# A prompt-and-sample decoder step: input rows and first norm in another order, the samples' depthwise convolution as 32x32 matmuls

## What is computed

```python
mods = (silu(c) @ w_ada + b_ada).reshape(B, N_MOD, D_MODEL)
...
h = modulate(x, norm_g[l, 0], m[:, 0], m[:, 1])
...
def conv_module(h, prev, w_pw1, b_pw1, w_dw, b_dw, ln_g, ln_b, w_pw2):
    a = h @ w_pw1 + b_pw1
    u = a[..., :D_MODEL] * jax.nn.sigmoid(a[..., D_MODEL:])
    up = jnp.concatenate([prev.astype(u.dtype), u], axis=1)
    y = lax.conv_general_dilated(up, w_dw[:, None, :].astype(up.dtype), (1,), 'VALID',
                                 dimension_numbers=('NWC', 'WIO', 'NWC'),
                                 feature_group_count=D_MODEL) + b_dw
    y = jax.nn.silu(layernorm(y, ln_g, ln_b))
    return y @ w_pw2, up[:, -(CONV_W - 1):]
```

## Time and profile before

| | us |
|---|---|
| median of 3 runs | 1905.48 (1901.27 to 1909.15) |
| the profiled execution | 1907.56 |
| its span, first to last instruction | 1905.9 |
| PE busy | 1679.4 |
| DVE busy | 914.8 |
| ACT busy | 561.5 |
| POOL busy | 270.9 |
| SP's DMA queue | 172.54 MB |

### The profile page before, as it was taken

The page is one execution under the profiler, slowest core; times in us unless marked ns, Lnnn a source line. Parts: engine busy times, 40 slices in busy tenths (PEclk is TensorE's granted clock), DMA queues, the critical chain, the costliest instruction groups (busy, mean ns, idle before and its releaser), DMA issues.

```text
span 1905.9 us, 30256 instructions
## 1 busy us (share of the span) xinstructions
PE 1679.4 (88%) x12409; PEld 1488.9 (78%) x12409; DVE 914.8 (48%) x1618; ACT 561.5 (29%) x1058; POOL 270.9 (14%) x384
## 2 busy tenths in 40 slices
PE   5788874497999999997988989988897999999995
PEld 2666653397999999997887965454497999999994
DVE  1479999755323232335224246756645323223333
ACT  2332221333222122222221355544423222122222
POOL 1002939120000000000210034432300000000000
PEclk8899987698999999998899999978998999999997
DMA  9399983051233222321322240020221233222311
GB/s 311 157 348 341 307 278 102 0 137 56 78 97 92 66 79 85 107 64 34 100 73 56 77 121 23 1 68 23 67 68 55 78 95 94 63 82 82 110 32 50
DMA packets 236591, 198.10 MB, mean 104 GB/s; under 512 B 6999, under 2 KB 196127, under 8 KB 236253
## 3 DMA queue, kind: packets, MB, share of 16 engines
q1 hardware_dynamic: 230448, 172.54, 29.4%
q0 software_dynamic: 5840, 23.30, 3.9%
q10 hardware_dynamic: 173, 0.39, 0.1%
HBM read 188.88 MB, written 11.20 MB: 105 GB/s over the span
## 4 chain that ended last, share of the span: by engine, by line
PE 71%; DVE 11%; issue 8%; ACT 4%; DMA 3%; DVEq 1%; POOL 1%; SPq 1%; ACTq 0%; POOLq 0%
PE ps L1444 58%; PE ps L1426 4%; PE ps L1752 2%; PE ps L1705 2%; DMA ada<-in_w_ada_dram 2%; DVE y L1117 2%; DVE wl L971 1%; PE ps L1631 1%; DVE r L1117 1%; PE ps L1472 1%; DVE r L995 1%; PE ps L1822 1%; DVE y L1122 1%; PE ps L1607 1%; DVE t L1005 1%
## 5 line engine op out<-in xcount | busy, mean ns | idle before, releaser
L1444 PE MATMUL ps<-Hh,wh 128*128 128x288 f32 x2128 | 470.8, 304 | 67.9 <-DVE Hl L1010 40.8
L1444 PE MATMUL ps<-Hl,wh 128*128 128x288 f32 x2128 | 465.4, 301 | 0.0
L1444 PE MATMUL ps<-Hh,wl 128*128 128x288 f32 x2128 | 464.2, 300 | 0.0
L646 ACT ACTIVATE wh<-raw 128x1024 fp32r<-128x1024 f32 (+1 forms) x173 | 192.9, 1116 | 828.2 <-PE ps L1444 805.8
L1444 PEld LDWEIGHTS ps<-Hh,wh 128*128 128x128 f32 x2128 | 351.5, 194 | 71.9 <-issue 70.5
L1444 PEld LDWEIGHTS ps<-Hl,wh 128*128 128x128 f32 x2128 | 351.9, 193 | 0.2
L1444 PEld LDWEIGHTS ps<-Hh,wl 128*128 128x128 f32 x2128 | 351.5, 193 | 0.2
L971 DVE TENSOR_TENSOR wl<-raw,wh 128x1024 fp32r<-128x1024 f32 (+1 forms) x173 | 225.1, 1301 | 255.5 <-ACT wh L646 255.0
L1444 PE MATMUL ps<-ah,wl 128*128 128x288 f32 x704 | 150.8, 296 | 0.0
L1444 PE MATMUL ps<-ah,wh 128*128 128x288 f32 x704 | 150.8, 296 | 0.0
L1444 PE MATMUL ps<-al,wh 128*128 128x288 f32 x704 | 150.7, 296 | 0.0
(11 more groups left out here) (273 smaller groups left out, 1958.5 us busy)
## 6 DMA issues: line engine op xcount, KB each, us to landing
ada<-in_w_ada_dram SPq DMA_DIRECT2D x64, 1024.0 KB, 7.6
raw<-in_ffn_w_up_dram SPq DMA_DIRECT2D x88, 512.0 KB, 3.8
raw<-in_ffn_w_down_dram SPq DMA_DIRECT2D x32, 704.0 KB, 4.6
raw<-in_conv_w_pw_dram SPq DMA_DIRECT2D x24, 512.0 KB, 8.5
raw<-in_w_kv_dram SPq DMA_DIRECT2D x12, 512.0 KB, 3.7
C<-in_cache_kv_dram POOLq DMA_DIRECT2D x32, 128.0 KB, 4.1
raw<-in_nsa_w_in_dram SPq DMA_DIRECT2D x8, 512.0 KB, 3.8
Cs<-in_cache_kv_dram SPq DMA_DIRECT2D x16, 256.0 KB, 3.9
```

The costliest lines, as they stand in the source:

```text
L646: A(wh[:, u % RING, 0:K, 0:w], raw[:, u % RING, 0:K, 0:w], ACT.Copy).then_inc(hi_ready, 1)
L1444: last = M(ps[0:w, 2 * s + h, 0:HT], wt[:, s, k, 0:w], rt[:, k, h * HT:(h + 1) * HT], start=(k == 0 and i == 0), stop=(k == K - 1 and i == 2))
```

## The change

**First stage.** Five row buffers in place of two (`ROW_BUF`, the new `xrows`), so that POOL issues all five blocks of x at once. The blocks of `state_conv` follow. PE turns all five blocks ahead of strip 0, and sums the squares between strip 0 and strip 1, into banks 4 and 5 (`stats0`) in place of 6 and 7. ACT's and DVE's first splits of weights move behind the blocks of x. `norm(0)` takes the reciprocal ahead of its wait for `mods`. The two copies from HBM to HBM (`conv_sample`, `win_sample`) move on POOL's queue behind the first unit of the second projection.

**Convolution.** `sel32` holds 1 where the partition is the column plus a multiple of 32. POOL builds, for each chunk, a tensor `taps_t[cc]` of 32 slots by 32 columns: slot k is `sel32` times tap k, so that each group of 32 partitions holds a 32x32 diagonal; slot 31 holds the bias and meets a row of ones. Chunks 0 and 1 are built early, into `stage`; 2 to 7, into the room of `Hh` and `Hl`, once PE has done the 16 units. PE then runs 32 x 32 x 64 matmuls, 4 partition groups x 4 column groups x 8 rounds for each chunk, 1024 in all; the four column groups take four taps at a time, the partition groups go to banks 0 to 3. ACT copies the four banks to `parts` (128x2048), four matmuls with `sel32` add the four column groups, and ACT puts the sum into y. PE's channel sums and DVE's subtraction wait for that (`cs_ev`).

Core of the diff:

```diff
-SMP_CONV = [(0, 4), (4, 7)]
+TAPS = CW + 1
+TAPS_EARLY = 2
...
-STRIP_BLOCKS = [1, 2, 3, 4]
+
+
+ROW_BUF = [0, 1, 2, 3, 4, 0, 1]
...
+        xrows = at("xrows", [P, 3, D], rH + DC * T * 4)
...
+        taps_t = [at(f"taps{cc}", [P, TAPS, 32], off_) for cc, off_ in enumerate(
+            [rG + 4096 * cc for cc in range(TAPS_EARLY)] + [rH + 4096 * cc for cc in range(DC - TAPS_EARLY)])]
+        parts = at("parts", [P, 4, 512], rH + 4096 * (DC - TAPS_EARLY))
+        assert 4096 * (DC - TAPS_EARLY) + 8192 <= 2 * DC * T * 4
...
             def load_rows(bk):
-                n = xi_rows[bk]
-                if bk >= 2:
-
-                    pool.wait_ge(S("xi_pe"), bk - 1)
+                if bk >= 5:
+                    pool.wait_ge(S("xi_pe"), bk - 4)
                 if bk < 4:
                     src = a["x_prompt"][0, bk * P:(bk + 1) * P, :]
                 elif bk == 4:
                     src = a["x_sample"].rearrange("b t d -> (b t) d")
                 else:
                     src = a["state_conv"].rearrange("l b t d -> (l b t) d")[120 * (bk - 5):120 * (bk - 4), :]
-                pool.dma_start(stage[0:n, bk % 2, :], src).then_inc(S(f"xi_in{bk % 2}"), 16)
-
-            load_rows(0)
-            load_rows(1)
+                pool.dma_start(rows_in(bk), src).then_inc(S(f"xi_in{ROW_BUF[bk]}"), 16)
+
+            for bk in range(5):
+                load_rows(bk)
             nc.gpsimd.memset(ones[:], 1.0).then_inc(S("const"), 1)
             nc.gpsimd.memset(epst[:], EPS).then_inc(S("const"), 1)
             nc.gpsimd.memset(cpad[:], 0.0).then_inc(S("const"), 1)
             nc.gpsimd.memset(u_p[:, :, 0:CW - 1], 0.0).then_inc(S("const"), 1)
-            for bk in range(2, 7):
+            for bk in range(5, 7):
                 load_rows(bk)
             pool.dma_start(pgt[:], a["page_table"].rearrange("b n -> (b n)").unsqueeze(0)).then_inc(S("pg_in"), 16)
 
+
+            pool.wait_ge(S("vec_dve"), 4)
+            pool.wait_ge(S("xi_pe"), 7)
+            for cc in range(DC):
+                if cc == TAPS_EARLY:
+                    pool.wait_ge(tile_done, U_PW2)
+                nc.gpsimd.tensor_tensor(taps_t[cc][:, 0:CW, :], sel32[:].unsqueeze(1).to_broadcast([P, CW, 32]),
+                                        wdT[:, cc:CW * DC:DC].unsqueeze(2).to_broadcast([P, CW, 32]),
+                                        ALU.mult).then_inc(S("taps_in"), 1)
+                nc.gpsimd.tensor_tensor(taps_t[cc][:, CW, :], sel32[:],
+                                        vT[:, R_BDW + cc:R_BDW + cc + 1].to_broadcast([P, 32]),
+                                        ALU.mult).then_inc(S("taps_in"), 1)
+
+            pool.wait_ge(tile_done, U_PW2 + 1)
+            pool.wait_ge(ada_ev, 16 * DC)
             pool.dma_start(o["conv_sample"][0, :, 0:CW - 1 - NT, :],
                            a["state_conv"][0, :, NT:CW - 1, :]).then_inc(S("thru"), 16)
             pool.dma_start(wss[:, 0:PAST, :], a["state_win"].rearrange("b s t h d -> b s (t h d)")).then_inc(S("thru"), 16)
-
-
-            ysmp = y[:, :, TP:T].rearrange("p c (b t) -> p c t b", b=NB)
-            fs4 = fs[:, :, :].rearrange("p c (t b) -> p c t b", b=NB)
-            pool.wait_ge(S("xi_act"), 7)
-            pool.wait_ge(S("xi_dve"), 7)
-            step, n = S("convs"), 0
-            for c0, c1 in SMP_CONV:
-                cs = slice(c0, c1)
-
-                def bc(col):
-                    return col.unsqueeze(2).unsqueeze(3).to_broadcast([P, c1 - c0, NT, NB])
-
-                pool.wait_ge(tile_free, 2 * c1)
-                nc.gpsimd.tensor_tensor(ysmp[:, cs], u_s[:, cs, 0:NT, :], bc(wdT[:, c0:c1]), ALU.mult).then_inc(step, 1)
-                pool.wait_ge(step, n + 1)
-                nc.gpsimd.tensor_tensor(ysmp[:, cs], ysmp[:, cs], bc(vT[:, R_BDW + c0:R_BDW + c1]), ALU.add).then_inc(step, 1)
-                for k in range(1, CW):
-                    nc.gpsimd.tensor_tensor(fs4[:, cs], u_s[:, cs, k:k + NT, :], bc(wdT[:, k * DC + c0:k * DC + c1]),
-                                            ALU.mult).then_inc(step, 1)
-                    pool.wait_ge(step, n + 2 * k + 1)
-                    nc.gpsimd.tensor_tensor(ysmp[:, cs], ysmp[:, cs], fs4[:, cs], ALU.add).then_inc(step, 1)
-                    pool.wait_ge(step, n + 2 * k + 2)
-                n += 2 * CW
-
-
-            pool.wait_ge(tile_done, U_PW2 + 1)
-            pool.wait_ge(ada_ev, 16 * DC)
...
-            for u in range(SPLIT_AHEAD):
-                split_hi(u)
...
             for bk in range(5):
                 block_out(bk)
-                if bk in STRIP_BLOCKS:
-                    if bk == STRIP_BLOCKS[0]:
-                        act.wait_ge(S("vec_dve"), 3)
-                    s_ = STRIP_BLOCKS.index(bk)
-                    strip_out(s_, s_ - 1 if s_ else None)
-            strip_out(None, STRIPS_FIRST - 1)
+            for u in range(SPLIT_AHEAD):
+                split_hi(u)
+            act.wait_ge(S("vec_dve"), 3)
+            strip_out(0, None)
             act.wait_ge(S("xi_dve"), 5)
             act.wait_ge(S("xi_act"), 5)
             for cc in range(DC):
                 A(sqb[:, cc, :], x[:, cc, :], ACT.Square).then_inc(S("st_sq"), 1)
             block_out(5)
+            strip_out(1, 0)
             block_out(6)
             root(0)
+            strip_out(2, 1)
+            strip_out(3, 2)
+            strip_out(None, STRIPS_FIRST - 1)
             norm_hi(0)
...
+            act.wait_ge(S("cs_pe"), 1)
+            A(parts[:], ps[:, 0:4, :], ACT.Copy).then_inc(S("cs_ev"), 1)
+            act.wait_ge(S("cs_pe"), 2)
+            A(y[:, :, TP:T].rearrange("p c (b t) -> p c t b", b=NB),
+              ps[:, 0, :].rearrange("p (c t b) -> p c t b", c=DC, b=NB), ACT.Copy).then_inc(S("cs_ev"), 1)
             act.wait_ge(S("cr_pe"), 1)
-            A(stage[0:CW - 1, 0, :].rearrange("p (b f) -> p b f", b=2), ps[0:CW - 1, 0:2, :], ACT.Copy).then_inc(S("cr_ev"), 1)
+            A(stage[0:CW - 1, 0, :].rearrange("p (b f) -> p b f", b=2), ps[0:CW - 1, 4:6, :], ACT.Copy).then_inc(S("cr_ev"), 1)
...
+                def inverse():
+                    dve.wait_ge(S("st_rms"), STAT_OF[k] + 1)
+                    V.reciprocal(r[:], r[:]).then_inc(S("st_r"), 1)
+
+                if k == 0:
+                    inverse()
...
-            for u in range(SPLIT_AHEAD):
-                split_lo(u)
+            V.tensor_reduce(sel32[:], ident[:].rearrange("p (g c) -> p c g", c=32), AX.X, ALU.add).then_inc(S("vec_dve"), 1)
             for bk in range(7):
+                if bk == 5:
+                    for u in range(SPLIT_AHEAD):
+                        split_lo(u)
...
-                if last:
-                    dve.wait_ge(tile_free, 2 * DC)
-                    V.tensor_scalar(acc_s, u_s[:, j, 0:NT, :], wj[0], vT[:, R_BDW + j:R_BDW + j + 1],
-                                    ALU.mult, ALU.add).then_inc(taps_s, 1)
...
-                        if last:
-                            dve.wait_ge(taps_s, i * per + k)
-                            V.scalar_tensor_tensor(acc_s, u_s[:, j, bass.ds(i * per + k, NT), :],
-                                                   wdT[:, bass.ds(i * (per * DC) + (k * DC + j), 1)], acc_s,
-                                                   ALU.mult, ALU.add).then_inc(taps_s, 1)
...
-            dve.wait_ge(S("convs"), 2 * CW * len(SMP_CONV))
+            dve.wait_ge(S("cs_ev"), 2)
             dve.wait_ge(taps, (CW + 1) * DC)
-            dve.wait_ge(taps_s, CW)
...
             def block_in(bk):
                 n = xi_rows[bk]
-                pe.wait_ge(S(f"xi_in{bk % 2}"), 16 * (bk // 2 + 1))
-                if bk >= 3:
-                    pe.wait_ge(S("xi_dve"), bk - 2)
-                    pe.wait_ge(S("xi_act"), bk - 2)
+                pe.wait_ge(S(f"xi_in{ROW_BUF[bk]}"), 16 * (1 + bk // 5))
+                if ROW_BANK[bk] in ROW_BANK[:bk]:
+                    before = max(k for k in range(bk) if ROW_BANK[k] == ROW_BANK[bk])
+                    pe.wait_ge(S("xi_dve"), before + 1)
+                    pe.wait_ge(S("xi_act"), before + 1)
                 for cc in range(DC):
-                    last = tr(ps[:, 2 * (bk % 3) + cc // 4, (cc % 4) * n:(cc % 4 + 1) * n],
-                              stage[0:n, bk % 2, cc * P:(cc + 1) * P])
+                    last = tr(ps[:, 2 * ROW_BANK[bk] + cc // 4, (cc % 4) * n:(cc % 4 + 1) * n],
+                              rows_in(bk)[:, cc * P:(cc + 1) * P])
                 last.then_inc(S("xi_pe"), 1)
 
             for bk in range(5):
                 block_in(bk)
-                if bk in STRIP_BLOCKS:
-                    s_ = STRIP_BLOCKS.index(bk)
-                    if s_ == 0:
-                        pe.wait_ge(S("const"), 4)
-                        pe.wait_ge(S("vec_act"), 1)
-                        pe.wait_ge(S("vec_dve"), 3)
-                    strip(s_)
-                    if s_:
-                        turn_strip(s_ - 1)
+            pe.wait_ge(S("const"), 4)
```

(51 more changed lines are left out.)

29 lines of the change are left out of this document (10 added, 19 removed).

## The result

The changed kernel takes 1929.2 us, the median of 7 runs (1915.74 to 1933.16), against 1909.15 for the kernel before on the same chip (7 runs, 1901.27 to 1910.4): a ratio of 1.0103, with an interval from 1.0072 to 1.0134. It is slower by 1%, where I had forecast 1876 and a gain. The profiled execution took 1929.2 us, with a span of 1927.5 against 1905.9.

The account below looks back on a forecast made before the run. DVE, perhaps also loads, was taken to hold the second stage, and something else, with 20.5 us of serial work, the first. Gains of 13 + 16.4 = 29.4 us off 1905.48 gave 1876 us; range 1848 to 1902.

Parts of the forecast that it names:

- the clock's rival: Convolution on PE: clock falls to 1.2 GHz, 52 ns a record, 106 us in all; about 1940 us; chance 0.14.
- 2.4 us lost: First stage: loss to PE's sums, extra blocks and the ring, set against a gain of 15.4, leaving 13 us.
- The serial part behind `mods`: First stage, from `mods` to PE's first dense matmul: 5.1 us in place of 20.5, a gain of 15.4.
- PE's waits in this stage cover most: First stage: PE's idle waits, 5.84 us ahead of the first half strip alone, absorb most of the added work.
- if at 65 or more, the ring ran dry: Sign for the first stage: PE's first dense matmul expected near 60 us rather than 73.1; 65 or more means a dry ring.
- if the sums are paid in full: First stage, lower bound of the gain: 15.4 - 9.6 = 6 us, with PE's channel sums wholly added.
- I take nothing for it: Second projection: the two moved HBM-to-HBM copies land where the DMA row stands at 0, 5 and 1; no cost.
- what would make the forecast wrong: Sign: a second projection lengthened by the two moved copies would make the forecast wrong altogether; no size given.
- The chunk of 24.04 and its relief: Second stage: a DVE chunk takes 24.04 us without POOL's sets and the small taps; 52 us off DVE.
- The pace: Second stage: loads hold DVE's chunks to one every 27.26 us, so chunk 7 starts at 280.5 rather than 274.2.
- 20 ns: Convolution on PE: time per record, the middle between 14 and 26 ns; 2048 records take 41 us, to 326.3.
- The tail: Behind the convolution: ACT's copies, `sel32` matmuls, hand-overs, all 16 channel sums and the mean, together 15.7 us, to 342.0.

Follow-up runs that it names:

- e6_sums_in_wait: e5_copies_mid with PE's first-stage channel sums between the two half strips of strip 0 and ACT's squares ahead of its strip 0 copy: 1911.65 us, 1.0022 of before.
- e10_spread_halves: e6_sums_in_wait with the samples' convolution spread over the second stage, 128 records ahead of each of units 3 to 15: 1869.8 us, 0.9839 of before.
- e7_spread: e5_copies_mid with the samples' convolution spread over the second stage, 256 records ahead of every other unit from 3 to 15: 1916.84 us, 1.0054 of before.
- e3_half_records: Changed kernel with its two HBM-to-HBM copies issued early and half of the convolution's matmuls left out, 1024 records in place of 2048: 1887.74 us.
- e5_copies_mid: Changed kernel with its two HBM-to-HBM copies issued behind POOL's last build of taps (296 us): 1916.13 us, 1.0067 of before.
- e9_shared: e6_sums_in_wait with the samples' convolution shared: chunks 2 to 6 on DVE, chunks 0, 1 and 7 on PE: 1890.47 us, 0.9926 of before.
- e12_copies_behind: Changed kernel with its two HBM-to-HBM copies issued behind the convolution, once ACT has written y: 1906.29 us, 0.9997 of before.

## Why the prediction was wrong, step by step

By my steps the mean should have come at 342.0 - 13 = 329.0. It came at 362.6, 33.6 us later: 7.6 from the first stage, 12.3 from the start of the convolution, 15.4 from its length, and -1.7 from the tail. Then 20.4 us in the second projection, for which I had taken nothing. The time came near the 1940 of the clock's rival by chance: the causes are others.

- **First stage: the term "2.4 us lost" measured 10.** The serial part behind `mods` was right: 67.70 - 62.45 = 5.3 against 5.1. But the last half strip came 9.9 us later. With "PE's waits in this stage cover most" I counted PE's time, where what counts is that a ring of three gets no new load while PE takes none; e6_sums_in_wait gave 5.3 of it back, and my own test ("if at 65 or more, the ring ran dry") said so at 67.70. Of the rest, PE's first transposes stood at 13.39 in place of 9.46, and SP issued its first load of `w_ada` at 13.09 in place of 9.82, beside the five row blocks that POOL now loads at once; no run took that apart. My lower bound of 6, "if the sums are paid in full", was nearly the result, 5.4.
- **The two copies: "I take nothing for it" measured 20.4.** I looked at the mean of the DMA row over slices of 48 us and found room. But within slice 9 the ring's next two loads are awaited at once, and a copy of megabytes ahead of them delays them to 35 us. I named this as what would make the forecast wrong, and gave it no price. The runs give one for each place: 12.6 us at the first dense matmul when issued at 20 (80.34 - 67.70), 12.3 under the convolution at 296, 20.4 at 401, none at 43 in the kernel before, at 341 there, or at 357.
- **DVE.** The chunk of 24.04 and its relief were right, and the last chunk took 31.3 us where I had 34.4. The pace was mis-sized: I took 27.26 us a chunk from a stretch in which 347 GB/s flowed (120 to 200 us), and got 29.0 (27.5, 30.9 and 28.6). Chunk 7 started 9.4 us later than my steps put it, counted from the first dense matmul, and the last strips took 2.9 more. Not all of it is the loads: in the window of the chunk of 30.9 (columns as above) the granted clock is 0.89, and 196 matmul records keep PE busy for 28.13 us, where as many took 25.14 at 1.00 in the 27.26 us that I read. The clock stood at 0.56 from 230 to 235 us, behind a wait of 2.41 us for a load.
```profile
225.00:256.00 31.00, 28.13 (x196) 20.19 (x192) 24.18 (x38) 7.79 (x24) 0.00 (x0) 0.89 0.93 316
```
- **The convolution: "20 ns" measured 27.5.** It was no rate. The records themselves cost 15.3 ns each, near the 14 of my nearest row, and a pause of 1.67 us on the average stands between runs of 128: 31.4 + 25.0 = 56.4 us. A row of 56 records could not show it.
- **The clock.** Of this rival one half held: the granted clock fell to 0.50. The other did not: the records were not slowed to 52 ns. 128 take 1.95 us at 0.50, and 1.5 at 1.00 in e10_spread_halves (there on eight tiles), so as an estimate the clock cost at most 7 us of the 56. It may have cost less, since a faster run may only have a longer pause: in e7_spread the visit at 323.54, whose first 114 records took 1.34 us, has a pause of 5.33, and the one at 175.58, whose first 115 took 1.84, one of 3.43. No run holds all else equal.
- **The tail** of 15.7 was 14.1. DVE waited 47 us for the mean rather than 27.
- **The cost of an instruction.** The Trainium skill, "TensorEngine Tiling (Array Packing)", section "Instruction Overhead", would have 25 ns a record. The measured 9.9 from start to start at a granted clock of 1.00 and 12.9 at 0.50 do not bear that out; the nearness of 27.5 is chance.

## What the pauses are

A record is a weight load and a matmul, two instructions, so a pause stands at every 256 instructions. The page's row of the DMA queue that carries instructions shows as much, before and after (packets, MB, share): 16 packets and 0.26 MB more, for 4096 more weight loads and matmuls, so one packet of 16 KB for each 256. There are 15 pauses. With half of the records (e3_half_records) the row has 106 packets, 8 more than before for 2048 instructions more.
```profile
q8 instruction: 98, 1.61, 0.3%
```
```profile
q8 instruction: 114, 1.87, 0.4%
```
From 292 to 349 us, the whole length of the convolution, the same row of the DMA view stands alone: the DMA engines move these 16 packets and nothing else.
```profile
q8 instruction: 16, 0.26, 2.0%
```
In the run that starts at 300.25 a packet moves between 301.0 and 301.5; the run is over at 302.2, and the next begins at 303.71. So the pause is not the packet's own time on the engines. From start to start the runs stand 3.45 to 4.00 us apart.

Four runs agree that PE waits for its own instructions there: pauses halve with the count (e3_half_records), grow when other transfers have the DMA engines (e5_copies_mid; also 3.24 and 4.52 us in e9_shared, at DMA shares of 0.64 and 0.37), come back to their size when these are gone (e12_copies_behind), and all but vanish when long matmuls stand between runs of 128 (e10_spread_halves). The Trainium skill describes this in "Advanced Engine Details and Errata", section "ISA Cache": lines of 256 instructions, and only two of them. The traces agree with both: a pause at each 256, and none in the first 215 records of the changed kernel, 430 instructions. The 128 KB that the section also gives for TensorE would be eight such lines; the traces do not bear that out. I had not read that section against 4096 short instructions in a row; with it the pause could have stood among the rivals, though its length of 1.5 to 2 us only the trace gives.

What stays open: how e7_spread's loss divides between its pauses (23.3 us), the clock at 0.50 behind each visit and the half strips not taken meanwhile. The spread in halves took away nearly all of the three together. Open too is what fills the 2.2 us from a packet to the next run.

## What to carry to other kernels

Where a stage is a long row of short instructions (here 7.6 ns each, two to a record), count instructions and not only their time, and put them in small groups between long ones: the same 2048 records cost 56 us in a row, and 31 us when spread, 21 in the 13 visits and 10.1 behind the last strip. The visits were not free: chunk 7 started 229.6 us behind the first dense matmul, against 216.8 in the changed kernel. A transfer of megabytes that nobody awaits still needs a place in which no load is awaited for its whole length; a mean over a slice doesn't show such a place, the next loads' issue times do. And a ring of buffers is fed by its consumer: work put between two of its takes costs what the loads lose.
